# The scan stage of a two-block transformer kernel: piece order query, two gates, value, output gate, with a head's mixer started at its second gate

## What is computed

```python
q, v, g, f_fwd, f_bwd = split(h @ w_in)            # 128 columns each per head, 8 heads; also for the context
q = silu(q)
f_d = lb_d + (1 - lb_d) * sigmoid(f_d); k_d = 1 - f_d; log_f_d = log(f_d)      # d = forward, backward
for chunk:                                          # S is the 128 x 128 state of one head
    b = cumsum(log_f); a[t, s] = sum_k q[t] * exp(b[t] - b[s]) * k[s]  (s <= t)
    o = a @ v + (q * exp(b)) @ S;  S = exp(b_end) * S + (k * exp(b_end - b)).T @ v
y = rms_norm(o_fwd + o_bwd, norm_g) * silu(g)       # then y @ w_o, added to x
```

## Time and profile before

| | us |
|---|---|
| median of 3 runs | 3711.52 (3711.49 to 3713.59) |
| profiled execution, its own time | 3712.82 |
| its span | 3711.0 |
| PE busy in the span | 3429.7 (92%) |
| DVE, ACT, POOL busy | 1809.2, 1252.3, 379.1 |
| first product of the scan stage's first piece | at 1218.08 |
| first product of the output projection | at 1771.85 |

### The profile page before, as it was taken

How to read it: one execution, slowest core, us unless ns; L and a number is a source line. 1 busy time by engine, 2 the same in 40 slices (tenths; PEclk the granted TensorE clock), 3 DMA queues, 4 the chain that set the end, 5 groups by cost and what they waited for, 6 DMA issues and landing times.

```text
span 3711.0 us, 42821 instructions
## 1 busy us (share of the span) xinstructions
PE 3429.7 (92%) x17064; PEld 2840.0 (77%) x17064; DVE 1809.2 (49%) x2729; ACT 1252.3 (34%) x1899; POOL 379.1 (10%) x384
## 2 busy tenths in 40 slices
PE   4999998999999898986899999999989999999898
PEld 3777777888888686875688878887768788877686
DVE  3665657855532577767433343343433433334333
ACT  2344443222212445443332233333332333333322
POOL 1010111000001133434000000001100000011000
PEclk7999989999999899998999999999999999999999
DMA  5222213566531111110233332222213222222132
GB/s 170 83 57 65 60 34 97 166 191 193 190 123 52 62 45 40 46 40 12 78 96 96 97 93 84 75 68 80 74 55 97 95 85 74 69 85 74 52 96 86
DMA packets 107974, 318.75 MB, mean 86 GB/s; under 512 B 28160, under 2 KB 29568, under 8 KB 107264
## 3 DMA queue, kind: packets, MB, share of 16 engines
q1 hardware_dynamic: 107776, 316.00, 27.5%
HBM read 313.86 MB, written 2.10 MB: 85 GB/s over the span
## 4 chain that ended last, share of the span: by engine, by line
PE 82%; DVE 9%; ACT 4%; issue 3%; DMA 1%; POOL 1%; SPq 0%; DVEq 0%; ACTq 0%
PE bank L901 20%; PE bank L903 20%; PE bank L902 20%; PE bank L906 3%; PE bank L907 3%; PE bank L908 3%; PE bank L1035 1%; PE bank L986 1%; PE bank L1088 1%; DVE tmp L1525 1%; PE bank L1107 1%; PE bank L1117 1%; PE bank L1070 1%; DVE h_low_lat L1531 1%; PE bank L1068 1%
## 5 line engine op out<-in xcount | busy, mean ns | idle before, releaser
L901 PE MATMUL bank<-h_high_lat,w_high 128*128 128x512 f32 x2752 | 1141.1, 415 | 75.1 <-DVE h_low_ctx L1531 35.0
L1479 DVE TENSOR_TENSOR w_low<-w_raw,w_high 128x1024 fp32r<-128x1024 f32 (+2 forms) x440 | 530.7, 1207 | 1184.2 <-ACT w_high L1165 1183.1
L903 PE MATMUL bank<-h_high_lat,w_low 128*128 128x512 f32 x2752 | 1086.0, 395 | 0.0
L902 PE MATMUL bank<-h_low_lat,w_high 128*128 128x512 f32 x2752 | 1086.0, 395 | 0.0
L1165 ACT CAST w_high<-w_raw 128x1024 fp32r<-128x1024 f32 (+2 forms) x440 | 451.1, 1027 | 1344.0 <-PE bank L903 861.4
L901 PEld LDWEIGHTS bank<-h_high_lat,w_high 128*128 128x128 f32 x2752 | 524.8, 191 | 197.6 <-issue 73.1
L903 PEld LDWEIGHTS bank<-h_high_lat,w_low 128*128 128x128 f32 x2752 | 524.4, 191 | 113.8
L902 PEld LDWEIGHTS bank<-h_low_lat,w_high 128*128 128x128 f32 x2752 | 525.8, 191 | 80.5 <-issue 8.0
L1491 DVE SCALAR_TENSOR_TENSOR ada_product<-w_raw,c_rows 128x1024 f32<-128x1024 f32 x192 | 246.6, 1284 | 65.1 <-DMA w_raw<-in_ada_w_dram 53.2
L906 PE MATMUL bank<-h_high_ctx,w_high 128*128 128x256 f32 x800 | 227.2, 284 | 0.0
L907 PE MATMUL bank<-h_low_ctx,w_high 128*128 128x256 f32 x800 | 227.0, 284 | 0.0
(11 more groups left out here) (251 smaller groups left out, 4520.9 us busy)
## 6 DMA issues: line engine op xcount, KB each, us to landing
w_raw<-in_w_in_dram SPq DMA_DIRECT2D x176, 512.0 KB, 3.6
w_raw<-in_ada_w_dram SPq DMA_DIRECT2D x88, 512.0 KB, 3.8
w_raw<-in_ffn_in_dram SPq DMA_DIRECT2D x88, 512.0 KB, 3.6
w_raw<-in_w_ada_dram SPq DMA_DIRECT2D x48, 512.0 KB, 4.5
w_raw<-in_hg_in_dram SPq DMA_DIRECT2D x40, 512.0 KB, 3.6
w_raw<-in_ffn_out_dram SPq DMA_DIRECT2D x32, 512.0 KB, 3.5
w_raw<-in_qkv_dram SPq DMA_DIRECT2D x24, 512.0 KB, 3.6
w_raw<-in_proj_ret_dram SPq DMA_DIRECT2D x16, 512.0 KB, 3.6
```

Of the source, the lines that this page charges most:

```text
L901: e.matmul(lat_b, a, h[:, k, :], start=start, stop=False)
L902: e.matmul(lat_b, a, l[:, k, :], start=False, stop=False)
L903: done = e.matmul(lat_b, b, h[:, k, :], start=False, stop=stop)
L1479: e.tensor_tensor(w_lo[n % 2][:, 0:w], raw[slot][:, 0:w], w_hi[n % 2][:, 0:w].bitcast(F32), ALU.subtract).then_inc(s_lo, 1)
```

## The change

The five pieces of a head come in the order q, f0, f1, v, g. The mixer starts when f1 is done (`after=2`), so that v and g of the same head and q, f0, f1 of the next lie beside it; it has 34 steps over 35 projection steps, or over 28 for the last head, of which 14 exist. Inside the mixer the events are spaced anew: three empty steps behind the gate, `hg_df` of level 0 ahead of `hg_b`, the key-sum product ahead of the transposes of v, four empty steps behind these. The output gate's sigmoid and product leave `hg_gate` for an event of their own (`hg_sg`), and the product with it leaves `hg_rd` for `hg_y`; both stand behind the next head's `hg_gate`, for the last head around its readout. VectorE multiplies q last in the gate. hg_v has one buffer instead of two, hg_k four instead of three. hg_rd writes into `y_lat` itself. The code of other stages is the same; the `interleave` edit gives them the same plan.

```diff
--- before.py
+++ after.py
@@ -184,12 +184,12 @@
 
-    def interleave(self, producers, mixers, chunks, tail=(), tail_chunks=0):
+    def interleave(self, producers, mixers, chunks, tail=(), tail_chunks=0, after=-1):
         for i, pieces in enumerate(producers):
-            beside = tail_chunks if tail and i == len(producers) - 1 else chunks
-            for j, p in enumerate(pieces):
-                last = j == len(pieces) - 1
-                p(then=(lambda i=i, beside=beside: self.start_background(*mixers[i], beside)) if last else None)
+            beside = tail_chunks if tail_chunks and i == len(producers) - 1 else chunks
+            starts = pieces[after]
+            for p in pieces:
+                p(then=(lambda i=i, beside=beside: self.start_background(*mixers[i], beside)) if p is starts else None)
...
@@ -241,26 +241,33 @@
         self.ev("hg_gate", i)
+        if i > 0:
+            self.ev("hg_sg", i - 1)
+            self.ev("hg_y", i - 1)
+        for _ in range(3):
+            yield
+        for d in range(2):
+            self.ev("hg_ln", i, d)
+            yield
+        self.ev("hg_df", i, 0)
+        for d in range(2):
+            self.ev("hg_b", i, d)
+            yield
+        yield
+        self.ev("hg_a", i, -1)
         yield
         yield
         self.ev("hg_vt", i, 0)
         self.ev("hg_vt", i, 1)
-        yield
-        for d in range(2):
-            self.ev("hg_ln", i, d)
-            yield
-        for d in range(2):
-            self.ev("hg_b", i, d)
+        for _ in range(4):
             yield
         for s in range(len(LEVELS) + LAG):
             if s >= LAG:
                 self.ev("hg_a", i, s - LAG)
-            if s < len(LEVELS):
+            if 1 <= s < len(LEVELS):
                 self.ev("hg_df", i, s)
             if 1 <= s <= len(LEVELS):
                 self.ev("hg_fa", i, s - 1)
-            if s == 1:
-                self.ev("hg_a", i, -1)
...
@@ -270,11 +277,14 @@
         yield
-        yield
+        if i == HG_HEADS - 1:
+            self.ev("hg_sg", i)
         self.ev("hg_o", i)
         yield
         yield
         self.ev("hg_rd", i)
+        if i == HG_HEADS - 1:
+            self.ev("hg_y", i)
...
@@ -349,7 +359,7 @@
                                                                  gate=("norm", 2) if i == 0 and b == 0 else None)
-                for b, name, rhs in ((0, "hg_q", "h"), (2, "hg_g", "h"), (3, "hg_f0", "hc"), (4, "hg_f1", "hc"), (1, "hg_v", "hc"))]
+                for b, name, rhs in ((0, "hg_q", "h"), (3, "hg_f0", "hc"), (4, "hg_f1", "hc"), (1, "hg_v", "hc"), (2, "hg_g", "h"))]
...
@@ -395,7 +405,8 @@
         self.ev("hg_init")
-        self.interleave([self.hg_pieces(i) for i in range(HG_HEADS)], [(self.hg_mixer(i), 24) for i in range(HG_HEADS)], 5 * (KC - 1))
+        self.interleave([self.hg_pieces(i) for i in range(HG_HEADS)], [(self.hg_mixer(i), 34) for i in range(HG_HEADS)], 5 * (KC - 1),
+                        tail_chunks=4 * (KC - 1), after=2)
...
@@ -496,9 +507,9 @@
             hg_q, hg_g = (ring(n, 2, [P, LAT], st) for n in ("hg_q", "hg_g"))
-            hg_v = ring("hg_v", 2, [P, TOK], st)
+            hg_v = sb("hg_v", [P, TOK], F32, st)
             hg_f = ring("hg_f", 3, [P, TOK], st)
-            hg_k = ring("hg_k", 3, [P, TOK], st)
+            hg_k = ring("hg_k", 4, [P, TOK], st)
...
@@ -1262,10 +1274,10 @@
                         i = p.epi[1]
-                        if i >= 2:
-                            e.wait_ge(s_hvt, 2 * (i - 1))
+                        if i >= 1:
+                            e.wait_ge(s_hvt, 2 * i)
                         e.wait_ge(s_mm, n + 1)
-                        e.copy(hg_v[i % 2][:, 0:LAT], lat_b).then_inc(s_la, 1)
+                        e.copy(hg_v[:, 0:LAT], lat_b).then_inc(s_la, 1)
...
@@ -1339,22 +1351,27 @@
                         n = by_epi[("hg_f%d" % d, i)]
-                        t, k = hg_f[use % 3], hg_k[use % 3]
-                        if use >= 3:
-                            e.wait_ge(s_ha, ha_last[(use - 3) // 2])
+                        t, k = hg_f[use % 3], hg_k[use % 4]
+                        if use >= 4:
+                            e.wait_ge(s_ha, ha_last[(use - 4) // 2])
                         e.wait_ge(*lat_free[n])
                         e.wait_ge(*ctx_free[n])
                         act(k[:, :], t[:, :], ACT.Sigmoid, scale=-1.0).then_inc(s_hk, 1)
                         act(t[:, :], t[:, :], ACT.Sigmoid).then_inc(s_hf, 1)
-                    for c, (x, name) in enumerate(((hg_q[i % 2], "hg_q"), (hg_g[i % 2], "hg_g"))):
-                        if i == 0:
-                            e.wait_ge(s_hm, 2)
-                        elif c == 0:
-                            e.wait_ge(s_hqg, 2 * i)
-                        else:
-                            e.wait_ge(s_hout, i)
-                        e.wait_ge(*lat_free[by_epi[(name, i)]])
-                        act(tmp[(3 * i + c) % 2][:, 0:LAT], x[:, :], ACT.Sigmoid).then_inc(s_hy, 1)
+                    if i == 0:
+                        e.wait_ge(s_hm, 2)
+                    else:
+                        e.wait_ge(s_hrd, i)
+                    e.wait_ge(*lat_free[by_epi[("hg_q", i)]])
+                    act(tmp[0][:, 0:LAT], hg_q[i % 2][:, :], ACT.Sigmoid).then_inc(s_hy, 1)
+                elif kind == "hg_sg":
+                    i = ev[1]
+                    if i == 0:
+                        e.wait_ge(s_hm, 2)
+                    else:
+                        e.wait_ge(s_hgg, i)
+                    e.wait_ge(*lat_free[by_epi[("hg_g", i)]])
+                    act(tmp[1][:, 0:LAT], hg_g[i % 2][:, :], ACT.Sigmoid).then_inc(s_hgy, 1)
...
@@ -1393,7 +1410,8 @@
                     i = ev[1]
-                    o = tmp[(3 * i + 2) % 2][:, 0:LAT]
+                    o = tmp[0][:, 0:LAT]
+                    e.wait_ge(s_hqg, i + 1)
...
@@ -1682,14 +1700,11 @@
                     i = ev[1]
-                    for c, x in enumerate((hg_q[i % 2], hg_g[i % 2])):
-                        e.wait_ge(s_hy, 2 * i + c + 1)
-                        e.tensor_tensor(x[:, :], x[:, :], tmp[(3 * i + c) % 2][:, 0:LAT], ALU.mult).then_inc(s_hqg, 1)
                     if i == 0:
                         e.wait_ge(s_lb, 2)
                     for d in range(2):
                         use = 2 * i + d
-                        t, k = hg_f[use % 3], hg_k[use % 3]
+                        t, k = hg_f[use % 3], hg_k[use % 4]
...
@@ -1700,7 +1715,18 @@
                     e.wait_ge(s_hkk, 2 * i + 2)
-                    e.tensor_tensor(hg_ks[:, :], hg_k[2 * i % 3][:, 0:LAT], hg_k[(2 * i + 1) % 3][:, 0:LAT], ALU.add).then_inc(s_hks, 1)
+                    e.tensor_tensor(hg_ks[:, :], hg_k[2 * i % 4][:, 0:LAT], hg_k[(2 * i + 1) % 4][:, 0:LAT], ALU.add).then_inc(s_hks, 1)
+                    e.wait_ge(s_hy, i + 1)
+                    e.tensor_tensor(hg_q[i % 2][:, :], hg_q[i % 2][:, :], tmp[0][:, 0:LAT], ALU.mult).then_inc(s_hqg, 1)
+                elif kind == "hg_sg":
+                    i = ev[1]
+                    e.wait_ge(s_hgy, i + 1)
+                    e.tensor_tensor(hg_g[i % 2][:, :], hg_g[i % 2][:, :], tmp[1][:, 0:LAT], ALU.mult).then_inc(s_hgg, 1)
+                elif kind == "hg_y":
+                    i = ev[1]
+                    e.wait_ge(s_hrd, i + 1)
+                    e.wait_ge(s_hgg, i + 1)
+                    e.tensor_tensor(YL[:, i, :], YL[:, i, :], hg_g[i % 2][:, :], ALU.mult).then_inc(s_hout, 1)
...
@@ -1772,12 +1800,9 @@
                     i = ev[1]
-                    o = tmp[(3 * i + 2) % 2][:, 0:LAT]
+                    o = tmp[0][:, 0:LAT]
                     e.wait_ge(s_hre, i + 1)
-                    e.scalar_tensor_tensor(o, o, v_col("hgn"), RS[:, 0:LAT], ALU.mult, ALU.mult).then_inc(s_dve, 1)
-                    own += 1
-                    e.wait_ge(s_dve, own)
-                    e.tensor_tensor(YL[:, i, :], o, hg_g[i % 2][:, :], ALU.mult).then_inc(s_hout, 1)
+                    e.scalar_tensor_tensor(YL[:, i, :], o, v_col("hgn"), RS[:, 0:LAT], ALU.mult, ALU.mult).then_inc(s_hrd, 1)
...
```

More of the change, by code:

```diff
@@ L665, in build @@
         s_hgo, s_hoc, s_hsq, s_hrs = sem("s_hg_o_bank"), sem("s_hg_o"), sem("s_hg_square"), sem("s_hg_stat_bank")
-        s_hl2, s_hre, s_hout = sem("s_hg_rstd_ln"), sem("s_hg_rstd"), sem("s_hg_y")
+        s_hl2, s_hre, s_hrd, s_hout = sem("s_hg_rstd_ln"), sem("s_hg_rstd"), sem("s_hg_normed"), sem("s_hg_y")
+        s_hgy, s_hgg = sem("s_hg_g_sig"), sem("s_hg_g")
         s_pos, s_ang, s_trig = sem("s_pos"), sem("s_angles"), sem("s_trig")
@@ L999, in _ @@
                     for j in range(4 if g == 0 else 2):
-                        done = e.transpose(b[:, j * P:(j + 1) * P], hg_v[i % 2][:, P * (4 * g + j):P * (4 * g + j) + P], IDENT)
+                        done = e.transpose(b[:, j * P:(j + 1) * P], hg_v[:, P * (4 * g + j):P * (4 * g + j) + P], IDENT)
                     done.then_inc(s_hvt, 1)
@@ L1025, in _ @@
```

(13 more changed lines are left out.)

## The result

| | before | changed |
|---|---|---|
| median of 14 runs each | 3713.16 us (3711.16 to 3716.03) | 3719.37 us (3717.56 to 3720.96) |
| ratio of the changed kernel to before | | 1.0017 (95% interval 1.0009 to 1.0025) |
| span of the profiled execution | 3711.0 | 3718.5 |
| f1 of head 0 ends | 1258.2 | 1252.2 |
| first product of the output projection | 1771.85 | 1779.41 |

The changed kernel is 6.2 us (0.17%) slower. The interval excludes no change, but the size is inside the 7.4 us that the prediction called the bound of a measurement. The forecast was 3720.0; the case "slower by over 0.2%", to which I gave 0.55, was missed by a hair. The 3720 had been counted from 3711.5, the median of three runs; the 14 runs here give 3713.2, and 8 us on that would have been 3721.

What follows compares the result with a forecast made beforehand. TensorE, busy 92% of the span, waits for operands behind VectorE's in-order queue. Stage end 1252.1 + 466.2 (seven heads) - 1.3 + 63.1 = 1780.1 against 1771.85, +8 us, on median 3711.5: 3720 us, range 3703 to 3737.

Steps and rivals of the forecast that it cites:

- slower by over 0.2%: Whole kernel: time per head P comes out above 66.5 us, slower than measurement can confuse with no change; chance 0.55.
- Head 0's start: Start of the scan stage's heads: f1 of head 0 ends at 1252.1 instead of 1258.2, without g ahead of it.
- The long wait: At v's transposes, once per head: TensorE stands still 11.2 us until VectorE has copied v's context half.
- The low clock behind it: TensorE's products just after its 11.2 us wait run at half clock, losing 1.9 us a head; bounds 0 and 3.8.
- The second wait: At the fifth level's product in each head: TensorE waits again, some 2.2 us; bounds 0 and 4.
- TensorE's own work: TensorE's work for one head without idle time or clock loss: 51.3 us, from 385.7 / 7 - 3.8.
- 0.94 costs 6% of 63.4: In the old kernel's heads: the granted clock of 0.94 costs TensorE 3.8 us of each 63.4 us head.
- P: New time per head, from f1's end to the next f1's end: 66.6 us forecast; both kernels equal at 65.2.
- The tail: From the last head's f1 end to the first output-projection product: 63.1 us, including one extra table load of 1.28.
- The chain inside it hardly changes: Last mixer: times counted from f1's end match the old ones from v's end, such as 26.5 us to the first level operand.
- The faster case: Heads: v's copy ready at T + 21 and no second wait, P 61.5, gain 27 us, 3684; chance of faster 0.18.
- The low clock at every wait: Heads: each wait brings half clock, P 70.3 at worst, likelier 3732; chance 0.15, shared with a tail not shortened.

## Why the prediction was right

- **Head 0's start:** 1252.1 forecast, 1252.2 measured. The last tenth is luck: in the profiled executions the stage began anywhere from 1215.6 to 1218.1, with the same code ahead of it. From the stage's first product to f1's end it was 34.0 forecast and 34.3 measured.
- **The long wait:** 11.2 us from T + 12.7 to T + 23.9 forecast; 11.35 from T + 12.5 to T + 23.9 measured. Laying the queues of three engines out from one event, with durations of rows, gave the end of the chain to 0.1 us. The prediction's cause is shown by two runs: with the decays behind v the wait falls to 2.6 us, and with only the transposes later it moves to q's weights.
- **The low clock behind it:** 1.9 us forecast. In head 4 the five products from 1542.37 took 2.16 us instead of 1.15 at full clock, and from the transposes' start to the next product it was 1.16 instead of 0.60 as in the kernel with the decays apart (1498.80 to 1499.40 there); together 1.6. But head 4 is a short case. The granted clock (third column from the end) and TensorE's busy time in the wait and behind it, in head 4 and then behind head 5's wait:

```profile
1529.86:1541.20 11.34, 0.00 (x1) 0.02 (x1) 9.52 (x13) 4.34 (x8) 6.99 (x8) 0.69 0.00 0
1541.20:1544.36 3.16, 3.15 (x11) 2.78 (x12) 0.50 (x1) 0.86 (x2) 0.00 (x0) 0.50 0.52 169
1607.27:1612.63 5.36, 5.35 (x16) 4.49 (x17) 0.51 (x1) 0.86 (x2) 0.00 (x0) 0.50 0.34 101
```

Heads 0, 2, 4 and 6 run 3.1 to 3.4 us at the low clock, heads 1, 3 and 5 run 5.3 to 5.6. At 0.50 of the full clock half of that time is lost: 1.6 to 2.8 us, 2.1 in the mean of seven. The 3.8 that I gave as the upper bound did not come.

- **The second wait:** at the fifth level's product, as forecast, 1.6 us instead of 2.2, at T + 47.0 instead of 47.5.
- **TensorE's own work:** 51.3 us a head forecast, 51.5 measured. The step "0.94 costs 6% of 63.4" counts idle time too. The sums over all stretches of the seven heads in which the granted clock was 0.50 show for how much of them TensorE was busy, before and then in the changed kernel:

```profile
sum 54.62, PE 49.69 PEld 42.16 DVE 50.87 ACT 25.38 POOL 39.72; mean PE 3.82 PEld 3.24 DVE 3.91 ACT 1.95 POOL 3.06
sum 81.94, PE 29.38 PEld 25.27 DVE 49.23 ACT 28.41 POOL 34.88; mean PE 4.20 PEld 3.61 DVE 7.03 ACT 4.06 POOL 4.98
```

Before, little of the low clock fell on idle time: the products lost half of 49.7 us, 3.5 a head, where the step had 3.8. In the changed kernel most of it does; they lost half of 29.4, 2.1 a head, and the same step would have taken off 9% of 66.3, 6.0. Less what they lost, TensorE's own work is 51.5 us a head in both kernels (55.1 - 3.5 and 53.6 - 2.1, rounded). So the step was harmless where it was used, and would not have been in the changed kernel.

- **P:** the six heads behind head 0 took 51.5 + 11.3 + 2.2 + 1.6 = 66.6 us, own work, long wait, low clock and second wait; 66.6 was forecast, as 51.3 + 11.2 + 1.9 + 2.2. The second wait was 0.6 too long and the other three terms together as much too short. The mechanism is the forecast one; that the total agrees to a tenth is luck.
- **The tail:** 63.1 forecast, 62.8 measured, with the extra table load on the chain as the prediction had it. The run with the gate between the levels shows it: its wait is 1.3 us less, its tail 0.9. From the mean square's product to the output projection's it was 7.07 us before (1764.78 to 1771.85) and 8.35 now (1771.06 to 1779.41), 1.28 more. The Trainium skill ("ScalarE: Activation LUTs", What ACT_TABLE_LOAD costs) would have put 1.4 us more there for a drain; in the trace the sigmoid starts 0.02 us behind the load's end, and the tail was no longer than the row's 1.28 made it. Here the measurement decides, against the page's figure. The good total hides two misses. "The chain inside it hardly changes" put the end of the first level's operand at T + 26.7, and it was T + 27.7, behind v's transposes. And from the first product of the mixer's output (`hg_o`) to the mean square's it took 1.4 us less, at the full clock, which the sum didn't have. The kernel before, then the changed one:

```profile
1758.89:1764.78 5.89, 4.40 (x25) 4.24 (x25) 0.00 (x0) 1.22 (x2) 0.00 (x0) 0.74 0.01 3
1766.60:1771.06 4.46, 2.92 (x24) 2.76 (x25) 0.42 (x1) 1.21 (x2) 0.00 (x0) 1.00 0.00 0
```

- **The rivals:** the measured P of 66.6 lies 0.1 above the point at which I had put "slower by over 0.2%", and yet the medians came out 1.2 us below it: the two cases were cut at a place where neither the forecast nor a measurement could part them. The faster case needed v's copy at T + 21; it ended at T + 23.8. The low clock at every wait did not come. And the change does do what it says: without the early start of mixer 7 the tail is 9.3 us longer.
- **The sum:** the stage from f1 of head 0 to f1 of head 7 was forecast at 464.9 us and took 464.4; +8 us in all forecast, the spans differ by 7.5 and the medians by 6.2.

What the prediction saw as one change is two with opposite signs. The new order by itself is a gain (3693.2 us with every mixer started late), and the early start a loss of 26 us on top, because the decays came to stand ahead of what TensorE needs next: a head is 4.8 us longer with the early start (66.3 against 61.5), and another order on the queues gave 5.2 back. Of the early start's own merit at least 9 us at the end are real; with the decays moved, the early start comes to 3681.6 and then 3663.8 us. Whether it then gains in the heads as well is not shown: they take 61.1 us with it and 61.5 with the late start, but the late start was only run with the decays in front, where they hold up f1's weights.

## What to carry to other kernels

When work is started earlier beside a saturated engine, write down what stands *behind* it on each in-order queue of the helpers: here 8.5 us of decays that could stand later held back a 0.4 us copy and a 1.2 us weight split that TensorE wanted at once. If a wait ends at a late tile, look for everything else that is late behind the same instructions before moving its reader: moved alone, the reader gave 2 us a head, the blocking work moved gave 5 and then, with the rest respaced, 8. And price a low clock by the time at it in which the engine is busy, not by the mean clock of a stretch with idle time in it.

## What was not expected of the hardware

The time that TensorE ran at the low of its two clocks did not go by the length of the wait before: behind 7.8 us products stood 0.43 us apart for 3.9 us, and behind waits of 11.3 us here the low clock lasted 3.1 to 3.4 us in some heads and 5.3 to 5.6 in others (heads 4 and 5 above), the transposes included. In the kernel with the decays apart, where the waits are 2.7 us and less, the granted clock of the stretch is 0.98. Why heads with the same wait differ, no run here shows.
